# One memory unit moved from the mixer's attention to the memory's attention, in a two-layer transformer kernel

## The reference, cut to what matters

```python
x = x + hybrid_mixer_2(rms_norm(x), ...)          # attention of 6 + 6 heads over the 256 tokens, a gated MLP, w_out
x = x + memory_cross_attention(rms_norm(x), mem)  # this one and the mixer are what the change touches
x = x + conv_gated_ffn(rms_norm(x), ...)

def memory_cross_attention(h, mem, mem_kv_norm, mem_w_q, mem_w_kv, mem_w_o):
    q  = (h @ mem_w_q).reshape(B, S, 4, 128)
    kv = rms_norm(mem, mem_kv_norm) @ mem_w_kv     # 1024 columns: 512 of keys, 512 of values; needs mem only, not x
    k, v = kv[..., :512], kv[..., 512:]            # 256 memory tokens, 4 heads of 128
    return block_attention(q, k, v, 128 ** -0.5) @ mem_w_o   # softmax(q k^T) v
```

## Time and profile before

| | us |
|---|---|
| median of 3 runs | 2320.65 (2319.68 to 2322.66) |
| the profiled execution | 2323.65 |
| its span (first to last instruction) | 2321.9 |
| PE busy | 2269.6 (98% of the span) |
| POOL busy | 1697.1 (73%) |
| ACT busy | 1087.5 (47%) |
| DVE busy | 1065.1 (46%) |

### The profile page before, as it was taken

One profiled execution on the slowest core, in us unless ns is written; L12 is line 12 of the kernel. 1 busy time (PEld: TensorE's weight loads), 2 busy tenths in 40 slices (PEclk: granted clock), 3 DMA queues, 4 the chain that ended last, 5 costly groups with the idle time before them and its releaser, 6 DMA issues.

```text
span 2321.9 us, 42212 instructions
## 1 busy us (share of the span) xinstructions
PE 2269.6 (98%) x16657; PEld 2070.1 (89%) x16657; DVE 1065.1 (46%) x1867; ACT 1087.5 (47%) x1311; POOL 1697.1 (73%) x1340
## 2 busy tenths in 40 slices
PE   8999999999999999999999999999999999999998
PEld 7888999999988888899999998889898888898887
DVE  3334756323333333465553333333635674534766
ACT  4335444465433433454444744345554335565333
POOL 6998655556899899784554679985468996655996
PEclk9999999999999999999999999999999999999999
DMA  7554533334555455543343445564234655333653
GB/s 241 191 196 149 161 110 110 119 113 140 168 196 192 165 199 197 173 155 110 110 128 92 145 164 182 191 204 135 96 128 146 199 182 160 123 105 114 199 193 123
DMA packets 312376, 360.02 MB, mean 155 GB/s; under 512 B 18661, under 2 KB 291105, under 8 KB 312097
## 3 DMA queue, kind: packets, MB, share of 16 engines
q1 hardware_dynamic: 311866, 357.59, 47.4%
q10 hardware_dynamic: 358, 0.33, 0.0%
HBM read 356.84 MB, written 1.05 MB: 154 GB/s over the span
## 4 chain that ended last, share of the span: by engine, by line
PE 89%; DVE 5%; ACT 3%; issue 1%; POOL 1%; DMA 0%; SPq 0%; DVEq 0%; ACTq 0%
PE ps L764 23%; PE ps L564 21%; PE ps L596 17%; PE ps L601 9%; PE ps L643 3%; PE ps L894 1%; PE ps L876 1%; PE ps L1145 1%; PE ps L659 1%; POOL sb_lo L537 1%; PE ps L897 1%; PE ps L630 1%; PE ps L1197 1%; PE ps L803 1%; PE ps L998 1%
## 5 line engine op out<-in xcount | busy, mean ns | idle before, releaser
L537 POOL TENSOR_TENSOR sb_lo<-sb_raw,sb_hi 128x512 fp32r<-128x512 f32 (+1 forms) x1336 | 1696.9, 1304 | 606.9 <-ACT sb_hi L1306 606.5
L1306 ACT ACTIVATE sb_hi<-sb_raw 128x2048 fp32r<-128x2048 f32 (+3 forms) x341 | 639.0, 1876 | 733.0 <-PE ps L601 349.4
L596 PE MATMUL ps<-sb_hT,sb_hi 128*128 128x512 f32 x1792 | 426.0, 390 | 0.0
L596 PEld LDWEIGHTS ps<-sb_hT,sb_hi 128*128 128x128 f32 x1792 | 332.7, 188 | 66.7
L764 PE MATMUL ps<-sb_hT,sb_hi 128*128 128x256 f32 x2304 | 309.0, 287 | 4.5 <-DVE sb_hT L2158 2.8
L764 PEld LDWEIGHTS ps<-sb_hT,sb_hi 128*128 128x128 f32 x2304 | 284.9, 191 | 10.6 <-DVE sb_hT L2158 3.2
L601 PEld LDWEIGHTS ps<-sb_hT,sb_lo 128*128 128x128 f32 x1792 | 229.8, 191 | 8.7
L601 PE MATMUL ps<-sb_hT,sb_lo 128*128 128x256 f32 x1792 | 232.4, 283 | 0.0
L1910 DVE TENSOR_TENSOR sb_yinv<-ps,sb_row 128x512 f32<-128x512 f32 x112 | 77.5, 692 | 334.9 <-PE ps L601 334.9
L564 PE MATMUL ps<-sb_hi,sb_o_h 128*128 128x512 f32 x560 | 219.6, 392 | 0.9 <-DVE sb_o_l L1917 0.9
L564 PE MATMUL ps<-sb_hi,sb_o_l 128*128 128x512 f32 x560 | 218.6, 390 | 0.0
(11 more groups left out here) (401 smaller groups left out, 3359.4 us busy)
## 6 DMA issues: line engine op xcount, KB each, us to landing
sb_raw<-in_ffn_w_in SPq DMA_DIRECT2D x88, 1024.0 KB, 5.1
sb_raw<-in_w_in SPq DMA_DIRECT2D x78, 1024.0 KB, 5.2
sb_raw<-in_ffn_w_out SPq DMA_DIRECT2D x44, 1024.0 KB, 4.9
sb_raw<-in_ffn_w_up SPq DMA_DIRECT2D x44, 1024.0 KB, 5.1
sb_raw<-in_ffn_w_down SPq DMA_DIRECT2D x22, 1024.0 KB, 4.9
sb_raw<-in_w_out SPq DMA_DIRECT2D x16, 1024.0 KB, 5.1
sb_raw<-in_w_branch_a SPq DMA_DIRECT2D x8, 1024.0 KB, 5.2
sb_raw<-in_w_branch_b SPq DMA_DIRECT2D x8, 1024.0 KB, 5.3
```

Of the source, the lines that this page charges most:

```text
L537: ins = nc.gpsimd.tensor_tensor(lo[:, slot, c], raw[:, slot, c], hi[:, slot, c].bitcast(F32), ALU.subtract)
L596: mm(ps[:, bank + i, :].rearrange("p (h n) -> p h n", h=2), wh[:, c, i * P:(i + 1) * P], hT_both[:, :, c, :], start=c == 0, stop=False, sk ...
L1306: fn(hi[:, slot, 0:width], raw[:, slot, 0:width], ACT.Copy).then_inc(hi_ready, 1)
```

## The change

Unit 12 (`mem_w_kv`, the values of head pair 1) becomes unit 18, behind the query units; `w_out` is now 12 to 15, `mem_w_q` 16 and 17. `MEM_PLAN` deals 12 parts instead of 16, with other weights: two at the start, one behind each of s0, s1, t1, v1, s3, t3, v3 and s5, two behind t5; none any longer behind v0, s2, v2, s4 and v4. In the memory's attention the 20 transposes of `warm` go; three parts of unit 18 stand in their place, ahead of PE's wait at t0, and the fourth stands behind t0. ACT takes unit 18 out right behind its copy pt0 and then splits unit 20, which it did in `enter` before. Since unit 18 reads the normed memory in `o_h`, `o_l`, the queries' input goes to two other buffers, which share the memory of `vT` and `levels`. The turned weights of t1 go to banks 2 and 3, since 6 and 7 are taken.

```diff
-MEM_WEIGHT = {"s0": 1, "s1": 2.9, "t0": 0, f"t{M2_BATCHES - 1}": 3, f"v{M2_BATCHES - 1}": 0}
+MEM_WEIGHT = {"s0": 1, "s1": 1, "t0": 0, "v0": 0.8, f"t{M2_BATCHES - 1}": 2, f"v{M2_BATCHES - 1}": 0}
-MEM_PLAN = plan(range(9, 13), [3] + [... else {"s": 1.5, "t": 0.3, "v": 1.5}[step[0]]
+OUT_UNIT, QUERY_UNIT, VALUE_UNIT = 12, 16, 18
+MEM_PLAN = plan(range(9, 12), [2] + [... else {"s": 0.6, "t": 0.3, "v": 0.6}[step[0]]
...
+        with nc.sbuf_tensor("sb_vT", [P, KB, S], F32) as vT:
+            pass
+        query_low = sb("query_low", [P, KB, S], F32R)
...
+        with nc.sbuf_tensor("sb_levels", [P, 4, 512], F32) as levels:
+            pass
+        query_high = sb("query_high", [P, KB, S], F32R)
...
@@ SP queue
+                load(b, VALUE_UNIT, cols("mem_w_kv_2", l, 768, 256), 8, 256)
...
@@ PE, memory
-                enter(..., ((17, 6), (18, 7)), MEMORY_BANKS, MEMORY_ROW, 3, src=oT)
+                enter(..., ((QUERY_UNIT, 6), (QUERY_UNIT + 1, 7)), MEMORY_BANKS, MEMORY_ROW, 3, src=query_in)
...
-                        pe.wait_ge(mem_kv, 4 * l + 4)
+                        pe.wait_ge(mem_kv, 4 * l + 2)
...
                         if beta == 0:
-                            warm(6)
+                            values = quarters(b, VALUE_UNIT, oT, 6, by_token=True)
+                            for _ in range(PARTS - 1):
+                                next(values)
+                        else:
+                            next(values)
                         wv(f"pn{beta}")
-                        weights_out((sqf, rsf)[beta % 2], 4 + bank).then_inc(me_pe, 1)
+                        weights_out((sqf, rsf)[beta % 2], (4, 2)[beta]).then_inc(me_pe, 1)
                     else:
                         wa(f"pt{beta}")
+                        pe.wait_ge(mem_kv, 4 * l + (3 + beta))
...
@@ ACT, memory
-                enter(..., lambda i: split(b, 19 + i), o_h)
+                enter(..., lambda i: split(b, 18 + i), query_in[0])
+
+                def values_out():
+
+                    done(b, VALUE_UNIT)
+                    fn(mem_v[:, :, S:2 * S], two(ps[:, 6, :]), ACT.Copy).then_inc(mem_kv, 1)
+                    split(b, 20)
```

More of the change, by code:

```diff
@@ L233 @@
 SB_PLAN = plan(numbers(SB_BG[0]), [3, 2, 0]) + plan(numbers(SB_BG[1]), 3 * SB_WEIGHT)
-MEM_WEIGHT = {"s0": 1, "s1": 2.9, "t0": 0, f"t{M2_BATCHES - 1}": 3, f"v{M2_BATCHES - 1}": 0}
+MEM_WEIGHT = {"s0": 1, "s1": 1, "t0": 0, "v0": 0.8, f"t{M2_BATCHES - 1}": 2, f"v{M2_BATCHES - 1}": 0}
 OUT_AT = 6
-MEM_PLAN = plan(range(9, 13), [3] + [MEM_WEIGHT[step] if step in MEM_WEIGHT else {"s": 1.5, "t": 0.3, "v": 1.5}[step[0]]
+OUT_UNIT, QUERY_UNIT, VALUE_UNIT = 12, 16, 18
+MEM_PLAN = plan(range(9, 12), [2] + [MEM_WEIGHT[step] if step in MEM_WEIGHT else {"s": 0.6, "t": 0.3, "v": 0.6}[step[0]]
                                      for step in scores_order(M2_BATCHES)])
@@ L281, in build_program @@
         kT = sb("kT", [P, KB, S])
-        vT = sb("vT", [P, KB, S])
+        with nc.sbuf_tensor("sb_vT", [P, KB, S], F32) as vT:
+            pass
+        query_low = sb("query_low", [P, KB, S], F32R)
         zT = sb("zT", [P, KB, S])
@@ L289, in build_program @@
         u_v, w_k, k_dec, q_dec = (quad[:, i, :] for i in range(4))
-        levels = sb("levels", [P, 4, 512])
+        with nc.sbuf_tensor("sb_levels", [P, 4, 512], F32) as levels:
+            pass
+        query_high = sb("query_high", [P, KB, S], F32R)
         xinv, plev, mlev, lmat = (levels[:, i, :] for i in range(4))
@@ L323, in build_program @@
         mem_v = quad[:, 2:4, :]
+        query_in = (query_high[:], query_low[:])
         def cc(name):
@@ L501, in _ @@
                 load(b, 8, rows("mla_w_ukv_2", l, 0, 128), 1, 768)
-                for m in range(4):
+                for m in range(3):
                     load(b, 9 + m, cols("mem_w_kv_2", l, 256 * m, 256), 8, 256)
                 for m in range(4):
-                    load(b, 13 + m, cols("w_out_2", l, 256 * m, 256), 8, 256)
+                    load(b, OUT_UNIT + m, cols("w_out_2", l, 256 * m, 256), 8, 256)
                 for m in range(2):
-                    load(b, 17 + m, cols("mem_w_q_2", l, 256 * m, 256), 8, 256)
+                    load(b, QUERY_UNIT + m, cols("mem_w_q_2", l, 256 * m, 256), 8, 256)
+                load(b, VALUE_UNIT, cols("mem_w_kv_2", l, 768, 256), 8, 256)
                 for m in range(2):
@@ L1132, in out_half @@
                 def out_half(m, p0, p1, between=None):
-                    high_arrived(b, 13 + m)
-                    wh, wl = weights(13 + m, KB, 256)
+                    high_arrived(b, OUT_UNIT + m)
+                    wh, wl = weights(OUT_UNIT + m, KB, 256)
                     for w, acts in ((wh, hT), (wl, hT[0:1])):
                         if w is wl:
-                            arrived(b, 13 + m)
+                            arrived(b, OUT_UNIT + m)
                         for t in range(ST):
@@ L1223, in mixer2 @@
                         pe.wait_ge(x_ready, 4 * n + (m - 1))
-                        for _ in quarters(b, 13 + m, hT, 4 + m % 2, by_token=True):
+                        for _ in quarters(b, OUT_UNIT + m, hT, 4 + m % 2, by_token=True):
                             pass
@@ L1232, in memory @@
                 n = 3 * l + (3 * DEPTH + 1)
-                enter(2 * l + 3 * DEPTH, n, q + 3, b, ((17, 6), (18, 7)), MEMORY_BANKS, MEMORY_ROW, 3, src=oT)
+                enter(2 * l + 3 * DEPTH, n, q + 3, b, ((QUERY_UNIT, 6), (QUERY_UNIT + 1, 7)), MEMORY_BANKS, MEMORY_ROW, 3, src=query_in)
+                values = None
                 for step in ME_ORDER:
@@ L1766, in mixer2, with attention @@
                 out_highs(2, 4)
-            def attention(order, wp, wv, sig, scale, pts, bank, after, last=None):
+            def attention(order, wp, wv, sig, scale, pts, bank, after, turned=None, turned_at=M2_BATCHES - 1):
                 for step in order:
@@ L1782, in attention @@
                         sig(fn(pts[w], ps[:, bank[w]:bank[w] + 2, :].rearrange("p b (k n) -> p (b k) n", n=S), ACT.Copy))
-                        if beta == M2_BATCHES - 1:
-                            last()
+                        if beta == turned_at:
+                            turned()
                     else:
@@ L1793, in memory @@
                 two = lambda v: v.rearrange("p (k n) -> p k n", n=S)
+                two_next(b, 14)
+                high_pair(q + 3, 0, gain2(V2_MEMX), query_in[0], MEMORY_BANKS[0])
                 two_next(b, 15)
-                high_pair(q + 3, 0, gain2(V2_MEMX), o_h, MEMORY_BANKS[0])
-                two_next(b, 16)
                 for g in range(1, 3):
-                    high_pair(q + 3, g, gain2(V2_MEMX), o_h, MEMORY_BANKS[g])
-                enter(2 * l + 3 * DEPTH, n, q + 3, gain2(V2_MEMX), MEMORY_BANKS, MEMORY_ROW, 3, lambda i: split(b, 19 + i), o_h)
+                    high_pair(q + 3, g, gain2(V2_MEMX), query_in[0], MEMORY_BANKS[g])
+                enter(2 * l + 3 * DEPTH, n, q + 3, gain2(V2_MEMX), MEMORY_BANKS, MEMORY_ROW, 3, lambda i: split(b, 18 + i), query_in[0])
+                def values_out():
+                    done(b, VALUE_UNIT)
+                    fn(mem_v[:, :, S:2 * S], two(ps[:, 6, :]), ACT.Copy).then_inc(mem_kv, 1)
+                    split(b, 20)
                 def out_high(beta):
@@ L1803, in out_high @@
                     sig(fn(o_h[:, 2 * beta:2 * beta + 2, :], two(ps[:, 2 * beta, :]), ACT.Copy))
-                for _ in attention(ME_ORDER, wp, wv, sig, lambda n: P ** -0.5, (kT[:, 4:8, :], zT[:, 0:4, :]), (4, 6), out_high):
+                for _ in attention(ME_ORDER, wp, wv, sig, lambda n: P ** -0.5, (kT[:, 4:8, :], zT[:, 0:4, :]), (4, 2), out_high, values_out, 0):
                     pass
@@ L1853, in _ @@
                 mixer2(l, b, q)
-                for r in range(13, 15):
+                for r in range(12, 14):
                     two_next(b, r)
@@ L2376, in mixer2 @@
                 for m in range(4):
-                    dve.wait_ge(unit_done, RING * b + (13 + m + RING + 1))
+                    dve.wait_ge(unit_done, RING * b + (OUT_UNIT + m + RING + 1))
                     c = slice(S * m, S * (m + 1))
@@ L2381, in mixer2 @@
                     if m >= 1:
-                        low_pair(q + 3, m - 1, gain2(V2_MEMX), o_h, o_l, MEMORY_BANKS[m - 1])
+                        low_pair(q + 3, m - 1, gain2(V2_MEMX), *query_in, MEMORY_BANKS[m - 1])
             def maxima(beta, wp, sig, dk):
@@ L2394, in memory @@
                 sig = lambda ins: ins.then_inc(me_dve, 1)
-                low_pair(q + 3, 3, gain2(V2_MEMX), o_h, o_l, MEMORY_BANKS[3])
+                low_pair(q + 3, 3, gain2(V2_MEMX), *query_in, MEMORY_BANKS[3])
                 dve.wait_ge(row_ready, 2 * l + (3 * DEPTH + 1))
                 for m in range(2):
-                    dve.wait_ge(unit_done, RING * b + (17 + m + RING + 1))
+                    dve.wait_ge(unit_done, RING * b + (QUERY_UNIT + m + RING + 1))
```

## The result

The change made the kernel slower: 2326.95 us (median of 7 runs, 2322.98 to 2332.01) against 2320.60 us (7 runs, 2318.58 to 2322.66), +6.35 us. The ratio is 1.0027, 95% interval 1.0017 to 1.0036. The time was forecast at 2323.5 in a range of 2317.5 to 2329.0: right way, inside the range, but more than twice the size, and next to the rival "more half clock" (2327.1).

A forecast was written before the change was run, and what follows sets the result against it. PE, busy 98%, was taken to bound the kernel. Mixer's attention -1.4, memory's attention +2.5 and clock +1.8 summed to +2.9 us, put on the median: 2323.5 us, range 2317.5 to 2329.

The forecast's parts named there:

- more half clock: Rival: stands at t1 and v4 make the clock fall at each of the four; 2327.1 us, chance 0.25.
- stand ahead of t1: Mixer's attention: PE's wait ahead of t1 grows from 1.57 to 3.1 us, as a part behind v0 goes.
- stand at v4: Mixer's attention: new PE idle of 2.1 us, v4 waiting for ACT's copy pt4 behind the split of unit 13.
- t1 to t5 at full clock: Mixer's attention: t5 comes 0.7 us earlier per iteration, -1.4 us for both.
- scores of the memory to the products, first iteration: Memory's attention, first iteration: v1 and the products queued behind it come later, +2.0 us.
- the same, second iteration, which had lost time to the clock: Memory's attention, second iteration: products start at 2116.5 instead of 2116.00, +0.5 us.
- wait at v1: Memory's attention: v1 is held 0.9 us by ACT's split of unit 20, ahead of the copy pt1.
- all of it without the clock: Whole kernel, only the queues counted: -1.4 + 2.5 = +1.1 us, 2321.8; as rival "clock untouched", chance 0.18.
- new buffers: Other buffers for the queries' input: same instructions and shapes, taken at 0 us.
- clock at t1: Mixer's attention, t1 to s2: half clock in both iterations, +1.8 us in the second; bounds 0 and 3.7.
- clock at v4: Mixer's attention: the new idle at v4 could halve the clock; taken at 0, bounds 0 and 1.8 us per iteration.
- t2 is held by one of POOL's pieces in DVE's way: Mixer's attention: the maxima's scaling waits for POOL's piece; t2 at 2035.2, 0.1 us earlier than before.

The follow-up runs named there:

- e2: The changed kernel with ACT's split of unit 13 behind the copy pt3 instead of behind the norms at v3: 2323.22 us, ratio to before 1.0007.
- e1: The changed kernel with 26 unread transposes ahead of PE's wait at t1 and 14 ahead of v4: 2321.48 us, ratio to before 1.0004.
- e6: The kernel before with only the queries' input moved to the two other buffers: 2321.07 us, ratio to before 0.9999.
- e9: The changed kernel with only the 26 unread transposes ahead of PE's wait at t1: 2324.49 us, ratio to before 1.0015.
- e10: The changed kernel with only the 14 unread transposes ahead of PE's wait at v4: 2324.23 us, ratio to before 1.0016.
- e3: The changed kernel with the split of unit 20 behind the copy pt1 instead of ahead of it: 2326.30 us, ratio to before 1.0025.
- e4: The changed kernel with the parts behind t1 and t3 both moved behind v0: 2317.73 us, ratio to before 0.9991.
- e7: The kernel before with 13 unread transposes in its 1.57 us stand ahead of t1: 2320.66 us, ratio to before 0.9999.

## Why the prediction was right, and where it was off

| step | forecast | measured |
|---|---|---|
| stand ahead of t1 | 3.1 us | 3.06, both iterations |
| stand at v4 | 2.1 us, from ACT's queue with the split in it | 1.86 and 1.85; gone with the split elsewhere (e2) |
| t1 to t5 at full clock, against 29.8 | -0.7 | -1.0 (28.8 in e1) |
| scores of the memory to the products, first iteration | +2.0 | +1.95 (13.40 to 15.35) |
| the same, second iteration, which had lost time to the clock | +0.5 | +0.3 |
| wait at v1 | 0.9 | 0.87, both iterations |
| all of it without the clock | +1.1 | +1.0 (e1 against before) |
| new buffers | 0 | 0 (e6) |
| clock at t1 | +1.8 in one iteration | 2.1 per fall in the profiles; 2.5 (e9) or 2.8 (e1 against e10) for both in the medians |
| clock at v4 | 0 | 1.5 to 3.1 per fall in the profiles; 2.7 (e10) or 3.0 (e1 against e9) for both in the medians |

Behind t1 the half clock cost nearly what the rows said: 2.0 us from t1 to s2 (2030.19 to 2034.51 is 4.32, against 2.36), where 1.84 was read.

The mechanism was right; the term "clock at v4" was mis-sized. The prediction took 0 "since the second iteration's 1.57 us didn't" make the clock fall. That was an argument from one stand in one profile, and the same profile had a fall after 1.1 us. The clock fell behind v4 in both iterations of the changed kernel's profile, of e3's and of e9's, and in neither of e4's with the same stand of 1.85 us. A stand makes a fall likelier, and it is no threshold in its length alone.

A second part of the miss: the fall at t1 was charged once, because the profile of before already had one in the first iteration, and the +2.9 found that way was put on the median. That fall was no free one. t2 and t5 of that iteration, to be set against t1 at 1652.29:

```profile
1662.88 1.04 PE L1049 MATMUL ps<-sb_const,sb_sq 128*128 128x128 f32 x8
...
1683.77 1.04 PE L1049 MATMUL ps<-sb_const,sb_rs 128*128 128x128 f32 x8
```

t1 to t2 took 10.6 us against 8.85 in the second iteration, and t1 to t5 31.5 against 29.8, with PE waiting ahead of t2 in neither. Of the four iterations in the profiles of before and e6 this is the only one with a fall there, and filling the stand changed nothing (e7). So for most executions both falls at t1 are likely new, and with 1.8 for each the prediction would have said 2325.3. How often the kernel before has such a fall no run counts. In the changed kernel PE is not the last one at t2, and the fall costs its full length all the same: t2 waits for s2, its maxima and its exponentials, and comes 10.7 us after t1 with the fall (both iterations of the changed kernel's profile and of e10's), 8.6 without (e1, e9). Two such falls are 4.2 us, more than the 2.5 to 2.8 between the medians. That is within the uncertainty, and clocks fall elsewhere too (e1's profile has 0.72 over 1944 to 1950 us); the runs don't settle it.

Two agreements are in part luck. The sum without the clock, +1.1, leaves only +0.5 to the memory's second iteration, since the profiled execution had lost time to the clock there. At full clock the steps give -1.0 in the attention and +1.95 in the memory, twice, +1.9 in all; the measured +1.0 lies between -1.2 and 3.0. And the rival's 2327.1 has 1.8 us for t1 and 3.6 for v4, where the medians have 2.5 to 2.8 and 2.7 to 3.0. (In the same rival, the first iteration has 4.2 us from t1 of the memory to the products, not 4.3, so that the addition is 1.7.)

That t2 is held by one of POOL's pieces in DVE's way is as forecast, 8.7 us after t1. In e1 it came after 8.6, with a scaling of 0.99 us. In the changed kernel the scalings took 1.24 and 0.53 us and t2 came after 10.7 both times, since both scalings ended with the third of POOL's four pieces; the stands ahead of t2, 1.33 and 0.63 us, differ by how long the clock was at half for PE's own work.

The Trainium skill, TensorE: Matmul & The Clock Gate, section "HAM oscillation — how this bites in real kernels", describes a kernel in which TensorE waits once per tile and starts each next tile at the lower clock. Its waits are longer than the 1.85 us at v4, so it doesn't say that these would do it. The profiles of the changed kernel, e3, e9 and e10 agree that falls recur at recurring stands, here at 3.06 and at 1.85 us; e4's profile, with 1.85 us twice and no fall, is against it.

## What to carry to other kernels

Filler work that leaves one place must be weighed against the latency chain there: with a quarter of the parts gone, what sets the time is the order in the queue of the engine that serves the chain (here one split ahead of one copy, 1.85 us). Deal the parts that are left by the stands in the trace, not by smooth weights: the same 12 parts were worth 9 us more behind the step where PE stood. And price a new stand of TensorE with the clock that it may lose as well as its length: a fall cost 1.7 us where PE's own work set the time (before) and 2.1 us where a latency chain ran through PE's steps (changed). Count the falls of several executions before one profile's falls are taken for the median's.

## What the runs showed of the hardware that was not expected

Two fillings of PE stands, with nothing computed, took 5.5 us off a kernel with 2270 us of PE work, though the changed kernel's mean granted clock was 0.992 in the profile, and 0.999 with the fillings: the tenths of the page's clock line show 9 throughout in both. How often the clock falls differs from one execution to the next. The seven runs of the changed kernel go from 2322.98 us at a clock of 0.996 to 2332.01 at 0.992, and e2's eleven form two groups: three runs at 2319.3 to 2319.8 us with 0.997, eight at 2322.9 to 2325.9 with 0.993 to 0.995. The spread from lowest to highest is 9.0 us in the changed kernel, 4.7 in e1, 4.5 and 2.8 in e9 and e10.
